# A product-key expert layer: 4 heads x 32 tokens on the partitions, V sums in column groups, and U and V gathered apart

## The chip, the core and the metric

The kernel runs on one core of a Trainium2 chip. The metric is the device time of one execution in microseconds. Everything is fp32 except one attention mask.

## What is computed

Two layers of a decoder trunk on 256 tokens of width 1024: layer 0 is attention (eight MLA heads, eight MoBA heads), layer 1 a conformer convolution (31 taps per channel), and each is followed by PEER, the expert layer that takes most of the time:

```python
q = (xc @ w_q).reshape(128, 8, 2, 128)
s = einsum('thcd,hcnd->thcn', q, subkeys)
s_top, i_top = lax.top_k(s, 16)
cand = s_top[:, :, 0, :, None] + s_top[:, :, 1, None, :]
cand_idx = i_top[:, :, 0, :, None] * 128 + i_top[:, :, 1, None, :]
best, pos = lax.top_k(cand.reshape(128, 8, 256), 16)
idx = take_along_axis(cand_idx.reshape(128, 8, 256), pos, axis=-1)
g = softmax(best)
u, v = u_tab[idx], v_tab[idx]
act = gelu(einsum('td,thkd->thk', xc, u))
return einsum('thk,thkd->td', g * act, v)
```

So every token picks 16 of 16384 experts for each of 8 heads, in both layers: 256 x 8 x 16 x 2 = 65536 pairs of a U row and a V row of 4 KB each, 537 MB that are read once.

## The kernel before

**Tiling.** The 256 tokens are two tiles of 128. An expert *phase* is one tile in one layer: phase 0 and 1 are tile 0 and 1 of layer 0, phase 2 and 3 those of layer 1. A phase has eight heads of 16 *slots*, 512 slots in all. In a slot the 128 partitions are the 128 tokens of the tile, for one head and one of its 16 choices.

**A slot.** GpSimd issues one indirect DMA (`gathers`, L394) that puts each token's row of 8 KB, U beside V, into one of eight buffers of `ring`. VectorE's `dots` (L1237) multiplies the U half with the normed tokens `xn` and sums it into a column of `dot`. ScalarE's `peer_slot` (all of ScalarE's work has L758) applies Gelu, scales it with the gate into `coef`, and scales the identity matrix by it into `diag`. TensorE (all of its matmuls have L407, transposes L413 and L642) multiplies `diag` with the V half, two matmuls of 512 columns, onto `ypsum`, 128 tokens by 1024 columns. Its completion (`ring_free`) lets GpSimd reuse the buffer. `ypsum` is seeded with the tile itself, and VectorE copies it back after 128 slots (`peer_end`, L1324).

**Routing of the next head.** During slots 0 to 3 of a head, TensorE and ScalarE make the next head's queries, their transpose and the key scores (`peer_q`, `peer_qT`, `peer_scores`); during slots 4 to 10 VectorE finds the top 16 and their indices (`route`, L1173 to L1229). SyncE loads one head's weights (1152 KB, `load_head`, L339) as soon as the scores of the head before are done; four heads of layer 1 are loaded once and kept for phase 3.

**What sets the order.** Every engine works through a list written by hand, slot by slot, and waits on semaphores. Work of the other layers is put beside the slots by their number: the second tile's attention beside phase 0 (`beside_attention`, attention head a in slots 25 + 3a to 27 + 3a, the output projection in slots 77 to 82), each tile's convolution beside phases 1 and 2 (`beside_conv`: gated input in slots 7 to 41, taps in slots 16 to 80, norm and output projection in slots 84 to 107), and the norm for the next phase in slots 108 to 111. Between phases all drains: the next phase's first head is routed in the last one.

**Start.** Until the first gather, the first tile's projection and attention run; then the first expert norm, head 0's queries and its route. Two projections of the second tile (`project(1, 1)`, `project(1, 3)`) read weights that lie in the ring and come after head 0's scores.

## Time and profile before

| | us |
|---|---|
| median of 3 runs | 1716.0 |
| lowest and highest | 1713.87, 1719.32 |
| span of the profiled execution | 1710.8 |
| busy: TensorE, VectorE, ScalarE, GpSimd | 1387.0, 1125.6, 727.0, 594.8 |
| first gather issued, first dot | 133.92, 139.58 |
| ends of phases 0 to 3 (copies of `ypsum`) | 563.4, 965.4, 1375.4, 1701.5 |

The span is that of one execution under the profiler; the runs are timed without it. An engine's busy time is the union of its instructions. DMA share is the mean busy share of 16 DMA engines, and PEclk the share of full speed that TensorE's clock was granted. In a row of the timeline, the last bracket is the idle time before the instruction and what ended it.

### The profile page before, as it was taken

The page shows a single profiled execution, that of the slowest core. Times are in us where ns is not written, and L with a number is a line of the kernel's source. Part 1 is how long each engine was busy: PE and PEld are TensorE (multiplying, and loading weights), DVE is VectorE, ACT ScalarE, POOL GpSimd, SP SyncE. Part 2 cuts the span into 40 slices and gives each one's busy share as a digit, 9 for nine tenths or more (in the row PEclk, how much of TensorE's full clock was granted, in tenths as well). Part 3 has the DMA queues.
Part 4 walks back from the last instruction along what each step waited for, and adds up shares of the span by engine and source line. Part 5 has one row for each costly group of instructions (what it writes and reads, how often), then busy time and mean ns, then how long its engine had stood idle before and what let it go on. Part 6 is the DMA issues. An engine that isn't in the chain of part 4 may idle for free.

```text
span 1710.8 us, 17886 instructions
## 1 busy us (share of the span) xinstructions
PE 1387.0 (81%) x4018; PEld 677.3 (40%) x4018; DVE 1125.6 (66%) x3165; ACT 727.0 (42%) x2049; POOL 594.8 (35%) x516
## 2 busy tenths in 40 slices
PE   6998977779587888877888888877877888888886
PEld 3554443434133454423333454433332433333332
DVE  3346746654467758988845758888855666667664
ACT  2313556653234445443443454533443444444442
POOL 0003433333234333433333423344422334544452
PEclk9999999999889999999999999999999899999999
DMA  9108988887999988999998988999988899999996
GB/s 393 43 29 333 421 356 339 318 302 288 426 418 421 421 333 327 362 364 386 400 360 323 421 345 319 362 376 372 378 349 352 345 409 422 423 421 422 412 423 275
DMA packets 82585, 606.81 MB, mean 355 GB/s; under 512 B 9552, under 2 KB 9936, under 8 KB 11600
## 3 DMA queue, kind: packets, MB, share of 16 engines
q0 software_dynamic: 73728, 536.90, 78.5%
q1 hardware_dynamic: 8208, 64.36, 9.2%
q10 hardware_dynamic: 576, 4.72, 0.7%
q8 instruction: 28, 0.46, 0.1%
q14 instruction: 45, 0.37, 0.1%
HBM read 604.89 MB, written 1.05 MB: 354 GB/s over the span
## 4 chain that ended last, share of the span: by engine, by line
PE 42%; DVE 24%; ACT 12%; issue 11%; DMA 8%; DVEq 1%; POOL 1%; SPq 0%; POOLq 0%; ACTq 0%
PE ypsum L407 25%; PE bank L407 8%; DVE ring L1237 8%; DMA ring<-table_dram,idx 8%; PE qpsum L407 7%; ACT L758 4%; DVE arena L1133 4%; ACT diag L758 2%; ACT coef L758 2%; PE spsum L407 1%; ACT gel L758 1%; ACT arena L758 1%; POOL ring L394 1%; DVE topi L1187 1%; DVE sc L1201 1%
## 5 line engine op out<-in xcount | busy, mean ns | idle before, releaser
L407 PE MATMUL ypsum<-ring,diag 128*128 128x512 f32 x2048 | 1021.4, 634 | 287.3 <-ACT diag L758 285.9
L394 POOL DMA_INDIRECT ring<-table_dram,idx x512 | 594.6, 1161 | 1088.3 <-PE ypsum L407 879.4
L1237 DVE CUSTOM_DVE_ANT_0 ring<-xns,ring 128x1024 f32<-128x1024 f32 x512 | 618.2, 1221 | 151.1 <-DMA ring<-table_dram,idx 146.3
L407 PEld LDWEIGHTS ypsum<-ring,diag 128*128 128x128 f32 x2048 | 377.3, 198 | 821.6 <-ACT diag L758 498.8
L758 ACT ACTIVATE gel<-dot 128x1 f32<-128x1 f32 x512 | 102.2, 200 | 524.4 <-DVE dot L1237 503.9
L758 ACT ACTIVATE diag<-ident,coef 128x128 f32<-128x128 f32 x512 | 205.6, 402 | 85.3 <-PE ypsum L407 59.0
L758 ACT ACT_TABLE_LOAD x130 | 166.8, 1283 | 14.9 <-PE bank L413 9.8
L758 ACT ACTIVATE coef<-gel,g_cur 128x1 f32<-128x1 f32 x512 | 150.7, 294 | 16.6
L1133 DVE SCALAR_TENSOR_TENSOR arena<-arena,cols 128x128 f32<-128x128 f32 x480 | 136.5, 347 | 3.4 <-DVE sc L1178 0.7
L1173 DVE MAX8 top<-sc 128x8 f32<-128x128 f32 x64 | 15.6, 285 | 120.1 <-ACT sc L758 120.1
L407 PE MATMUL qpsum<-head,xns 128*128 128x256 f32 x384 | 86.9, 379 | 0.0
L407 PEld LDWEIGHTS qpsum<-head,xns 128*128 128x128 f32 x384 | 73.2, 191 | 20.7 <-issue 12.0
L758 ACT ACTIVATE qq<-qpsum 128x256 f32<-128x256 f32 x32 | 12.3, 385 | 135.5 <-PE qpsum L407 135.5
L407 PEld LDWEIGHTS bank<-hT,arena 128*128 128x128 f32 x512 | 60.0, 192 | 8.7 <-issue 8.7
L407 PE MATMUL bank<-arena,hT 128*128 128x512 f32 (+1 forms) x136 | 59.4, 580 | 0.9 <-ACT hT L758 0.9
L407 PE MATMUL bank<-hT,arena 128*128 128x128 f32 x512 | 59.7, 275 | 0.0
L1237 DVE DVE_READ_ACCUMULATOR2_ANT dot<- 128x1 f32 x512 | 42.3, 83 | 0.0
L1092 DVE TENSOR_SCALAR arena<-bank,arena 128x64 f32<-128x64 f32 x32 | 9.1, 284 | 47.1 <-PE bank L407 46.9
L407 PEld LDWEIGHTS bank<-arena,hT 128*128 128x128 f32 x136 | 26.4, 195 | 32.1 <-issue 30.6
L413 PE MATMUL bank<-ident,arena 128*128 128x128 f32 (+1 forms) x170 | 28.7, 290 | 11.9 <-DVE arena L1032 8.6
L758 ACT ACTIVATE arena<-bank 128x512 f32<-128x512 f32 (+3 forms) x31 | 16.5, 572 | 50.8 <-PE bank L407 48.6
L1086 DVE COPY arena<-bank 128x128 f32<-128x128 f32 (+1 forms) x32 | 11.4, 355 | 40.6 <-PE bank L413 40.5
(132 smaller groups left out, 858.3 us busy)
## 6 DMA issues: line engine op xcount, KB each, us to landing
head<-heads_dram SPq DMA_DIRECT2D x24, 1152.0 KB
ring<-w_in_dram SPq DMA_DIRECT2D x4, 2048.0 KB, 15.7
ring<-table_dram,idx POOLq DMA_INDIRECT x512
arena<-c_in_dram SPq DMA_DIRECT2D x4, 2048.0 KB, 26.4
arena<-heads_dram SPq DMA_DIRECT2D x4, 1152.0 KB
arena<-w_out_dram SPq DMA_DIRECT2D x1, 4096.0 KB, 36.6
arena<-c_out_dram ACTq DMA_DIRECT2D x2, 2048.0 KB, 9.8
xns<-gains_dram SPq DMA_DIRECT2D x5, 512.0 KB, 8.1
```

What stands on the lines that cost most here:

```text
L394: pool.indirect_dma_start(out=ring[:, b * 2 * D:(b + 1) * 2 * D], out_offset=None, in_=table[:, :], in_offset=bass.IndirectOffsetOnAxis(ap ...
L407: return nc.tensor.matmul(o_, l, r, start=start, stop=stop, **kw)
L413: last = nc.tensor.transpose(bank[0:rows_, i * P:(i + 1) * P], s, ident[:, :])
L758: return nc.scalar.activation(out_, in_, func, **kw)
L1086: free(j, V.tensor_copy(pT[a % 2][:, 0:t + 1, :].rearrange("p s t -> p (s t)"), banks[bank_no(j)][:, 0:(t + 1) * P]))
L1092: free(j, V.tensor_scalar(o[:, a * VD:(a + 1) * VD], banks[bank_no(j)][:, 0:VD], rinv[:, a:a + 1], None, ALU.mult))
L1133: own.did(V.scalar_tensor_tensor(out=acc[:, c, :], in0=uT[:, c, bass.ds(k + t * P, P)], scalar=cols[:, bass.ds(k + (C_TAPS + c * TAPS), 1) ...
L1173: own.did(V.max(top_[:, c, 0:8], sc_[:, c, :]))
L1187: own.did(V.max_index(topi_[:, c, 8:16], top_[:, c, 8:16], sc2_[:, c, :]))
L1201: own.then(V.match_replace(cand2[:, :], best[:, 0:8], cand[:, :], low))
L1237: V.tensor_tensor_reduce(out=u, in0=xn[p % 2], in1=u, scale=1.0, scalar=0.0, op0=ALU.mult, op1=ALU.add, accum_out=dot[:, k:k + 1]).then_in ...
```

## The change

1. **Partitions.** A *round* is 16 slots in which the partitions hold 4 heads x 32 tokens. A *group* is 32 tokens, two rounds (heads 0 to 3, then 4 to 7); a phase has four groups, and again 128 slots. The normed tokens are replicated four times for each group: TensorE multiplies them with a 0/1 matrix `rep` into two banks, and ScalarE copies these to `xnr`.
2. **V sums.** ScalarE scales a 128x32 piece of `gident` by the Gelu value into `wts`. `gident` holds the gate times a 32x32 identity under each head; VectorE makes it twice a round (`gates`, eight choices each). `coef` and the copy of the gates fall away. TensorE multiplies each `wts` with four pieces of 256 columns of the V rows, and puts piece j on partitions 32j to 32j+31 of `ypsum`, which so sums the heads as well. Two halves of `ypsum` alternate between groups; ScalarE writes each group back (`take_group`), and VectorE's copy falls away.
3. **Gathers.** `table` becomes `u_table` and `v_table`. A slot has two indirect DMAs of 128 rows of 4 KB. The U ring has six buffers, each free after its dot (`dot_ready`); the V ring has eight, each free after its sum (`v_free`).
4. **Heads.** A round needs the scores of four heads, so all eight heads' queries, transposes and scores are made ahead of a phase: for phase 0 before its first slot, otherwise beside slots 97 to 114 of phase 0 and 107 to 124 of phases 1 and 2, two slots apart. ScalarE copies them, by 32x256 pieces, to where each round's 128 rows lie together. SyncE loads a head in three pieces, each behind the wait that frees its place. Seven heads of layer 1 are kept instead of four.
5. **Beside the slots.** Gated input moves to slots 8 to 64 in halves, taps to slots 17 to 89 by pairs of channel blocks instead of fours, norm and output projection to slots 91 to 103, the next norm to slots 94 and 104. The first gather waits for the three projections whose weights lie in the ring. All loops are unrolled. The second half of the convolution's output weights is loaded by SyncE.

The diff, cut to its core:

```diff
@@ GpSimd
-            def gathers(p, h, last_chunks=False):
-                for k in range(TOPK):
-                    if k % RING == 0:
-                        pool.wait_ge(routed[k // RING], h + (p * HEADS + 1))
-                    b = k % RING
-                    pool.wait_ge(ring_free, h * TOPK + (p * SLOTS + k + 1))
-                    settle(pool)
-                    pool.indirect_dma_start(
-                        out=ring[:, b * 2 * D:(b + 1) * 2 * D], out_offset=None, in_=table[:, :],
-                        in_offset=bass.IndirectOffsetOnAxis(ap=idx[k // RING][:, b:b + 1], axis=0)).then_inc(row_in[b], 16)
+            for n in range(ALL_SLOTS):
+                R, k = divmod(n, TOPK)
+                if k == 0:
+                    pool.wait_ge(routed, R + 1)
+                if n == 0:
+                    for c in (1, 2, 3):
+                        full(pool, PROJ_JOB[1][c])
+                at_ = bass.IndirectOffsetOnAxis(ap=idx[R % 2][:, k:k + 1], axis=0)
+                held(pool, dot_ready, n - U_RING + 1)
+                settle(pool)
+                pool.indirect_dma_start(out=u_row(n), out_offset=None, in_=u_table[:, :], in_offset=at_).then_inc(u_in[n % U_RING], 16)
+                held(pool, v_free, n - V_RING + 1)
+                pool.indirect_dma_start(out=v_row(n), out_offset=None, in_=v_table[:, :], in_offset=at_).then_inc(v_in[n % V_RING], 16)
@@ TensorE
-            def peer_slot(H, k, stop=False):
-                pe.wait_ge(diag_ready, H * TOPK + (k + 1))
-                b = k % RING
-                for half in range(2):
-                    last = mm(ypsum[:, half * CHUNK:(half + 1) * CHUNK], diag[:, (k % 2) * P:(k % 2 + 1) * P],
-                              ring[:, b * 2 * D + D + half * CHUNK:b * 2 * D + D + (half + 1) * CHUNK], False, stop,
+            def add_slot(n):
+                G = n // GROUP_SLOTS
+                pe.wait_ge(v_in[n % V_RING], 16 * (n // V_RING + 1))
+                pe.wait_ge(wts_ready, n + 1)
+                w = wts[:, n % WTS * QT:(n % WTS + 1) * QT]
+                for j in range(QUAD):
+                    last = mm(y_of(G, j), w, v_row(n, slice(j * DQ, (j + 1) * DQ)), False, n % GROUP_SLOTS == GROUP_SLOTS - 1,
                               skip_group_check=True)
-                last.then_inc(ring_free, 1)
+                last.then_inc(v_free, 1)
+            def replicate(G):
+                for j, half in zip(rep_jobs(G), range(2)):
+                    bank = bank_of(pe, j)
+                    g = G % GROUPS
+                    mm(bank[:, :], rep[:, g * P:(g + 1) * P], xn[:, half * CHUNK:(half + 1) * CHUNK], True, True)\
+                        .then_inc(bank_full[bank_no(j)], 1)
+            def beside_heads(p, s):
+                if s == NORM_SLOT[p - 1] + 2:
+                    turn_input(p)
+                for h in range(HEADS):
+                    H, a = p * HEADS + h, s - head_slot(p, h)
+                    if a == 2:
+                        head_scores(H)
+                    if h == 2 and a == 0:
+                        replicate(p * GROUPS)
+                    if a == 0:
+                        head_queries(H)
+                    if a == 1:
+                        head_turn(H)
@@ TensorE, ahead of slot 0
+            turn_input(0)
+            head_queries(0)
+            head_turn(0)
+            head_queries(1)
+            head_scores(0)
...
+            head_turn(3)
+            head_scores(3)
             project(1, 1)
             project(1, 3)
+            for h in range(4, HEADS):
+                head_queries(h)
+                if h > 4:
+                    head_scores(h - 1)
+                head_turn(h)
+            head_scores(HEADS - 1)
@@ SyncE
+            def load_head(H):
+                layer, h = H // (TILES * HEADS), H % HEADS
+                held(sp, head_taken, H)
+                sp.dma_start(head[:, 0:HEAD_A], heads_in[layer][:, h * HEAD_W:h * HEAD_W + HEAD_A]).then_inc(head_a_in, 16)
+                if H:
+                    full(sp, q_job(H - 1))
+                sp.dma_start(head[:, HEAD_A:HEAD_K], heads_in[layer][:, h * HEAD_W + HEAD_A:h * HEAD_W + HEAD_K]).then_inc(head_b_in, 16)
+                if H:
+                    full(sp, s_job(H - 1))
+                sp.dma_start(head[:, HEAD_K:HEAD_W], heads_in[layer][:, h * HEAD_W + HEAD_K:(h + 1) * HEAD_W]).then_inc(keys_in, 16)
@@ ScalarE
-                own.then(run(coef[:, k:k + 1], gel[:, k:k + 1], scale=g_cur[:, k:k + 1]))
-                if not (first and k < 2):
-                    act.wait_ge(ring_free, H * TOPK + (k - 1 + RING))
-                run(diag[:, (k % 2) * P:(k % 2 + 1) * P], ident[:, :], scale=coef[:, k:k + 1]).then_inc(diag_ready, 1)
+                if k == 0:
+                    act.wait_ge(gates_ready, 2 * R + 1)
+                if k == TOPK // 2:
+                    act.wait_ge(gates_ready, 2 * R + 2)
+                if n >= WTS:
+                    act.wait_ge(v_free, n - WTS + 1)
+                run(wts[:, n % WTS * QT:(n % WTS + 1) * QT], gident[:, k * QT:(k + 1) * QT], scale=gel[:, k:k + 1]).then_inc(wts_ready, 1)
@@ VectorE
                 if part_ == 0:
-                    dve.wait_ge(s_copied, H + 1)
+                    emptied(dve, s_job(p * HEADS + (r % PER_GROUP + 1) * QUAD - 1))
+            def gates(R, half):
+                if half == 0:
+                    dve.wait_ge(exp_ready, R + 1)
                     own.then(V.reciprocal(e_inv[:, :], e_sum[:, :]))
+                m = TOPK // 2
+                if R:
+                    dve.wait_ge(wts_ready, (R - 1) * TOPK + (half + 1) * m)
+                V.scalar_tensor_tensor(
+                    out=gident[:, half * m * QT:(half + 1) * m * QT].rearrange("p (k t) -> p k t", k=m),
+                    in0=ident32[:, :].unsqueeze(1).to_broadcast([P, m, QT]), scalar=e_inv[:, 0:1],
+                    in1=e_g[:, half * m:(half + 1) * m].unsqueeze(2).to_broadcast([P, m, QT]),
+                    op0=ALU.mult, op1=ALU.mult).then_inc(gates_ready, 1)
```

## Rows read from the trace of the kernel before

**Rows 1.** The page: busy us of each engine, and GB/s in 40 slices
```profile
PE 1387.0 (81%) x4018; PEld 677.3 (40%) x4018; DVE 1125.6 (66%) x3165; ACT 727.0 (42%) x2049; POOL 594.8 (35%) x516
GB/s 393 43 29 333 421 356 339 318 302 288 426 418 421 421 333 327 362 364 386 400 360 323 421 345 319 362 376 372 378 349 352 345 409 422 423 421 422 412 423 275
```
**Rows 2.** Stretches: start:end length, busy us (instructions) per engine, PEclk, DMA share, GB/s
```profile
213.00:388.00 175.00, 132.98 (x402) 66.91 (x400) 100.94 (x276) 104.43 (x237) 56.56 (x50) 0.95 0.87 329
388.00:425.00 37.00, 36.87 (x104) 18.57 (x105) 13.79 (x27) 10.95 (x39) 10.16 (x10) 1.00 0.74 281
425.00:563.40 138.40, 102.19 (x231) 42.76 (x229) 80.89 (x213) 50.92 (x154) 51.35 (x45) 0.90 1.01 420
563.40:965.40 402.00, 329.74 (x1012) 164.62 (x1012) 299.42 (x860) 176.79 (x493) 147.14 (x128) 0.97 0.93 366
617.00:812.00 195.00, 157.74 (x471) 77.55 (x470) 170.85 (x518) 85.65 (x235) 72.83 (x63) 0.95 0.91 355
864.00:965.40 101.40, 84.45 (x217) 38.52 (x215) 58.80 (x153) 36.59 (x112) 37.03 (x33) 0.98 0.91 358
965.40:1375.40 410.00, 333.48 (x1012) 165.98 (x1012) 299.03 (x860) 176.67 (x493) 146.47 (x129) 0.95 0.91 358
1375.40:1701.50 326.10, 272.36 (x670) 121.12 (x670) 216.96 (x532) 139.86 (x440) 147.99 (x121) 0.98 0.99 412
```
**Rows 3.** Groups by form: line, engine, operation, tiles, shape, count, busy us, mean ns
```profile
L407 PE MATMUL ypsum<-ring,diag 128*128 128x512 f32 x2048 | 1021.4, 634 | 287.3 <-ACT diag L758 285.9 <-issue 0.6
L1237 DVE CUSTOM_DVE_ANT_0 ring<-xns,ring 128x1024 f32<-128x1024 f32 x512 | 618.2, 1221 | 151.1 <-DMA ring<-table_dram,idx 146.3 <-DVE pos L1210 1.1 <-DVE arena L1045 0.4
L394 POOL DMA_INDIRECT ring<-table_dram,idx x512 | 594.6, 1161 | 1088.3 <-PE ypsum L407 879.4 <-DVE idx L1222 133.5 <-issue 75.4
L758 ACT ACTIVATE diag<-ident,coef 128x128 f32<-128x128 f32 x512 | 205.6, 402 | 85.3 <-PE ypsum L407 59.0 <-ACT coef L758 0.2
L758 ACT ACTIVATE coef<-gel,g_cur 128x1 f32<-128x1 f32 x512 | 150.7, 294 | 16.6
L1133 DVE SCALAR_TENSOR_TENSOR arena<-arena,cols 128x128 f32<-128x128 f32 x480 | 136.5, 347 | 3.4 <-DVE sc L1178 0.7 <-DVE sc L1201 0.7 <-DVE pos L1210 0.7
L407 PE MATMUL qpsum<-head,xns 128*128 128x256 f32 x384 | 86.9, 379 | 0.0
L1194 DVE TENSOR_TENSOR sc<-top 128x256 f32<-128x256 f32 x32 | 13.4, 418 | 0.0
```
**Rows 4.** Two stretches: 8 KB gathers in phase 3; the output's 4 KB rows alone
```profile
1400.00:1430.00 30.00, 27.22 (x72) 13.31 (x71) 17.97 (x36) 14.84 (x47) 12.74 (x12) 0.94 1.01 422
1708.00:1711.00 3.00, 0.00 (x0) 0.00 (x0) 0.00 (x0) 0.00 (x0) 0.00 (x0) 0.50 0.43 175
```
**Rows 5.** Timeline, start us and us: a free issue; then dots and a held one
```profile
135.29 0.94 POOL L394 DMA_INDIRECT ring<-table_dram,idx  x1 [0.30 <-issue]
...
1498.02 1.23 DVE L1237 CUSTOM_DVE_ANT_0 ring<-xns,ring 128x1024 f32<-128x1024 f32 x1 [1.17 <-DMA ring<-table_dram,idx]
1498.45 1.59 POOL L394 DMA_INDIRECT ring<-table_dram,idx  x1 [0.78 <-PE ypsum L407]
1500.50 1.23 DVE L1237 CUSTOM_DVE_ANT_0 ring<-xns,ring 128x1024 f32<-128x1024 f32 x1 [1.25 <-DMA ring<-table_dram,idx]
```
**Rows 6.** The chain of work that ended last, beside attention: start us, us
```profile
279.95 0.41 ACT diag L758
...
280.41 1.98 PE ypsum L407 x4
```
**Rows 7.** Timeline of the start: head 0's queries, the first gather
```profile
117.82 3.62 PE L407 MATMUL qpsum<-head,xns 128*128 128x256 f32 x16
...
133.92 1.07 POOL L394 DMA_INDIRECT ring<-table_dram,idx  x1 [133.46 <-DVE idx L1222]
```
**Rows 8.** The loads of the gains (512 KB, L335): time to landing
```profile
DMA to landing us min/median/max: 3.6/8.1/9.5
```

More of the change, by code:

```diff
@@ L194, in build @@
         sel = sb("sel", 2 * TOPK)
[L195 removed]
+        idx = [sb(f"idx{i}", TOPK, u32) for i in range(2)]
         nbest = sb("nbest", 1)
@@ L261, in held @@
         def held(eng, signal, count):
-            if not (isinstance(count, int) and count == 0):
+            if count > 0:
                 eng.wait_ge(signal, count)
@@ new lines, in head_turn, with head_scores @@
+            def head_turn(H):
+                take(t_job(H), q_T, 2 * P)
+            def head_scores(H):
+                p, h = divmod(H, HEADS)
+                hq, i = divmod(h, QUAD)
+                held(act, routed, (p - 1) * ROUNDS + (GROUPS - 1) * PER_GROUP + hq + 1)
+                j = s_job(H)
+                full(act, j)
+                for g in range(GROUPS):
+                    last = run(scores_of(g * PER_GROUP + hq, slice(i * QT, (i + 1) * QT)), banks[bank_no(j)][g * QT:(g + 1) * QT, 0:2 * KEYS])
+                free(j, last)
```

759 lines of the change are left out of this document (378 added, 381 removed).

## The prediction

> **What bounds the kernel now.** I read the page's busy times first [rows 1]: no engine is full, TensorE leads with 81%, and the slices of the DMA run from 29 to 426 GB/s. So the limit changes with the stage, and the second view is the table of stretches [rows 2]. A slot gathers 128 rows of 8 KB (1.049 MB), makes one dot, one weight matrix and one accumulation; there are 512, in four expert phases of 128. The reader is to see three kinds of stage. (a) DMA at 412 to 422 GB/s: the last 45 slots of phase 0 and all of phase 3, where a slot takes 326.1/128 = 2.55 us. (b) Slots 25 to 72, beside attention: 175 us at 329 GB/s, 3.65 us a slot, no engine full; the three compute engines wait for each other in a ring. (c) The tap slots of phases 1 and 2: 195 us for 63 gathers, 3.10 us a slot, with 170.85/63 = 2.71 us of it busy VectorE. TensorE is the limit only in a short piece (388 to 425 us, busy 36.87 of 37). The 1021 us that TensorE spends on ypsum [rows 3] are thus mostly not time that can be won.
>
> **The transfers.** The bytes of a slot stay, in two halves with 4 KB rows. 8 KB gathers fill the DMA at 422/1.01 = 418 GB/s; the 4 KB rows of the output ran at 175/0.43 = 407 [rows 4]. That is a store and a short stretch, but the nearest row: 2.48 us between two dots of a full DMA [rows 5] become 2.48 x 418/407 = 2.55, and with the second completion I take 2.57. Ends: 2.49 (no loss) and 2.70.
>
> **Issuing on GpSimd.** 512 issues become 1024. A free one takes 0.94 us after a gap of 0.30 [rows 5]: two are 2.48 us, just below 2.57. But the issue at 1498.45 took 1.59 us: it began during a dot (1498.02 to 1499.25) and ended 0.79 us after that dot. The mean of all is 1.161 us [rows 3], and twice 1.46 is 2.92 us a slot, above the DMA. Which holds? A U issue waits for a dot's end (`dot_ready`), so it starts as the dot stops: about 0.8 + 0.3, then V's start at 1.1 us, before the next dot (2.57 - 1.23 = 1.34 us after the last), then the next U is held until that dot ends. Two issues fit each dot if nothing slips. I take 2.60 us a slot, nearer the free price because a full ring hides single slips; the other end, 2.92, is a rival.
>
> The row shows the issue held by the dot; the Trainium skill (SBUF — State Buffer, "Who interferes with whom") says that a VectorE instruction with two SBUF inputs contends with a GpSimd one that reads SBUF, and that the second fully blocks. By that rule, the trace agrees. The rule speaks against doubling the issues; it would not choose between 2.60 and 2.92.
>
> **The V sums.** Removed: two fp32 matmuls of 512 columns, 1.98 us a slot [rows 6]. Added: four of 256 columns onto 32 partitions each. One after another they cost four times 86.9/192 = 0.453 us = 1.81; side by side 0.45 [rows 3]. No row uses column groups; I take 0.9, between, and keep both. It counts only where TensorE stands in the ring. Off the path it lifts 1021 us to some 460.
> The Trainium skill (TensorEngine Tiling (Array Packing), "Theoretical Speedup") allows up to fourfold for 32 columns. By it the slot would cost the lower 0.45 and my total fall by about 10 us; no row here shows it.
>
> **ScalarE and VectorE.** `coef` (0.294 us) goes, `diag` (0.402) becomes a scale of 128x32 at perhaps 0.3 [rows 3]: 0.4 us less of each slot's chain. Sixteen replications and the copies of scores and outputs lie beside the DMA. VectorE gains two gate multiplications a round (32 rounds, 0.42 us each by a route's 128x256 operations [rows 3]: 0.05 us a slot) and loses small work; 1.22 us for a dot stays.
>
> **Start.** Now the first head's queries start at 117.82 and the first gather at 133.92 [rows 7]. After, round 0 needs heads 0 to 3. SyncE loads each head in three parts, each queued behind a wait for the head before, and TensorE waits in line: load 4 us, queries 3.6, scores 0.6, 8 us a head for three more; then both remaining projections end before the first gather. I get 160, 26 us later. Then TensorE must finish heads 4 to 7 before its first accumulation, with loads that share the DMA (a 512 KB gain landed in 3.6 to 9.5 us [rows 8]): about 10 us for each of three, to 196. VectorE stops at slot 4, since round 1 wants head 7's scores, and GpSimd stops at its eighth V buffer. From 196, 21 slots x 2.57 put slot 25 at 250, against 213 before: 37 us lost.
>
> **Phase 0, rest.** Slots 25 to 72: a head's ring takes three slots, 175/16 = 10.9 us. It passes one accumulation (1.98 to 0.9) and two to three weighings (0.4 each): 10.9 - 2.2 = 8.7, times 16 = 139 us (before 175). Slots 73 to 82: ten accumulations less by 1.1: 37 becomes 27. Last 45 slots: 47.2 MB of gathers, 10.7 of convolution weights, and now all eight heads of the next phase (9.4 MB, of which the earlier kernel loads two or three here): 67.3 MB at 0.41 MB/us = 164 us, less 10 that full rings hold in store, plus 6 for the chained loads: 160 (before 138.4). Phase 1 starts at 250 + 139 + 27 + 160 = 576 (before 563.4).
>
> **Phases 1 and 2.** First 17 slots at 2.60: 44. Taps now fill 73 slots at 3.4 instead of 3.9 a slot; a tap costs 136.5/480 = 0.284 us [rows 3]. VectorE busy 2.71 - 0.15 + 0.05 = 2.61, with small gaps 2.77: 202 us. Pairs instead of fours stall nothing, as two taps (0.57) outlast one tap's 0.347. Last 38 slots: 39.9 MB, 9.4 of heads, 2.1 of output weights: 125 us, less 10 in store; plus 19 because norm, convolution output and next queries now stand within 17 slots: that chain is about 41 us of work against 44 of transfers, and already ran at 358 GB/s [rows 2]. Phase 1: 44 + 202 + 115 + 19 = 380 (402). Phase 2 has seven kept heads beside its taps (DMA 188 + 20 = 208) and streams no heads at its end: 44 + 208 + 99 + 18 = 369, say 370 (410).
>
> **Phase 3.** 128 x 2.60 = 333 (326.1): a loss of 7. Tail 10 (9.3).
>
> **Sum.** 576 + 380 + 370 + 333 + 10 = 1669 us of span, against 1710.8. The span of the profiled execution lies 5.2 us under the median of the runs, 1716.0 (1713.87 to 1719.32); with about the same around it the time is 1675 us. What is won is 36 us beside attention, 10 in the mixing slots and 62 in the convolution phases; 37 go at the start, 22 at the end of phase 0 and 7 in phase 3.
>
> **Rivals.** (1) GpSimd becomes the bound: mean issues of 1.46 us. For it speaks that the mean issue, 1.161 us, stands 0.22 over a free one though issues now come only once a slot; against it, the lock step above. Price 0.32 us in 128 slots of phase 3 (41), 34 opening slots of phases 1 and 2 (11), 38 closing ones (12), 21 at the start (7), and 0.15 in 146 tap slots (22): 93 us, so 1768, slower. It decides from 2.60 + 0.32 x 41/93 = 2.74 us a slot on. (2) The column groups run one after another: 1.81 instead of 0.9 in 16 rings and 9 mixing slots, 23 us: 1698. TensorE would still not bind: 1.81 is below 2.57. Should the granted clock, 0.98 in phase 3 [rows 2], fall to 1.2 GHz because TensorE has less to do, side-by-side sums of 0.9 us do not bind either. (3) The chained head loads cost 12 us a head rather than 8 at the ends of phases 0 and 1: 16 x 4 = 64 us, 1739, slower; a full V ring (eight slots, 20 us) speaks against it. (4) The added losses of the start and the chains are hidden by rings filled ahead: 1635.
>
> **How the numbers follow.** Forecast 0.44 at 1675; (1) 0.24, (2) 0.12, (3) 0.10, (4) 0.10. All of the forecast, (2) and (4) are faster, 0.66; (1) and (3) are slower but for mild forms near the old time: same 0.06, slower 0.28. A change within 0.3% can't be told from none here. The range, 1630 to 1765, leaves out the fringes of (1) and (4).
>
> **What would show it.** First gather near 160 and first accumulation near 196; in phase 3, dots 2.6 us apart with the DMA above 400 GB/s (right) or 2.9 apart with GpSimd never idle and issues of 1.4 us (rival 1); four matmuls ending within 0.5 to 1 us or over 1.8; slots 25 to 72 in about 139 us; tap slots 2.77 us with VectorE above 90% busy. Most wrong would be a 4 KB gather that moves at well under 400 GB/s, or a start that loses more than 37 us.

## The result, and the profile of the changed kernel

The changed kernel took 1877.4 us (median of four runs, 1864.5 to 1885.3) against 1717.5: a ratio of 1.0918, interval 1.0881 to 1.0955. I had forecast 1675 with a range of 1630 to 1765, and a gain. The same program, measured twice more, took 1803.0 us (1796.4 to 1809.7; ratio 1.0492, 1.0438 to 1.0546) and 1892.5 (1878.1 to 1907.8; 1.1038, 1.0957 to 1.1119). Its run of 1907.8 us counts as slow, and the other three have a median of 1881.0. So the loss has two parts: one of about 85 us that is there each time, and one of 74 to 78 us that was there in two of three measurements. The second and third were made on chips 3 and 12; the chip of the first isn't on record.

The page of the changed kernel, its busy times and its 40 slices of DMA:

```profile
PE 1032.3 (55%) x6242; PEld 489.3 (26%) x6242; DVE 1146.1 (61%) x3162; ACT 616.0 (33%) x1699; POOL 1179.0 (63%) x1028
GB/s 383 15 48 198 256 349 339 341 338 371 415 396 370 369 334 314 352 286 357 363 322 368 372 321 309 335 337 410 404 378 243 301 344 367 356 355 373 350 341 282
```

Against [rows 1], TensorE is down by 355 us, and GpSimd is up from 594.8 to 1179.0. The last eight slices, 409 to 423 GB/s in the kernel before except for the last (275), are at 282 to 373. The groups behind it (line, engine, operation, count, busy us, mean ns of one, then the idle time before them):

```profile
L429 POOL DMA_INDIRECT ring<-u_table_dram,idx x512 | 582.8, 1138 | 410.8 <-issue 324.1
L431 POOL DMA_INDIRECT ring<-v_table_dram,idx x512 | 596.0, 1164 | 270.0 <-issue 137.6
L436 PE MATMUL ypsum<-ring,wts 128*32 128x256 f32 x4096 | 479.7, 552 | 723.7 <-ACT wts L792 425.8
```

The stretches of the changed kernel, cut at slots 0, 25, 73 and 82 of phase 0, at the first dots of phases 1, 2 and 3, and at the last dot (the third row so holds nine of the ten mixing slots 73 to 82, the fourth the tenth and the 45 behind it):

```profile
185.00:283.00 98.00, 54.18 (x312) 27.69 (x312) 57.44 (x168) 31.39 (x91) 57.20 (x49) 0.73 0.86 306
283.00:431.00 148.00, 97.75 (x546) 39.85 (x546) 99.63 (x268) 85.75 (x180) 111.55 (x96) 0.56 0.94 339
431.00:455.00 24.00, 21.13 (x101) 8.62 (x102) 13.41 (x27) 7.42 (x24) 19.06 (x17) 0.78 0.98 367
455.00:622.00 167.00, 90.17 (x576) 47.56 (x578) 85.96 (x218) 52.68 (x160) 89.68 (x88) 0.72 1.01 395
622.00:1050.00 428.00, 234.95 (x1502) 116.97 (x1494) 305.06 (x860) 143.60 (x386) 302.06 (x254) 0.68 0.93 340
1050.00:1486.00 436.00, 243.50 (x1599) 126.33 (x1596) 305.80 (x859) 150.94 (x411) 303.23 (x259) 0.68 0.92 339
1486.00:1863.00 377.00, 146.71 (x1114) 37.90 (x1106) 220.06 (x529) 98.71 (x320) 284.62 (x251) 0.54 0.96 356
```

and of the same program where it took 1803 us, its three last phases:

```profile
615.00:1024.00 409.00, 231.11 (x1504) 116.50 (x1494) 305.68 (x859) 144.45 (x387) 300.63 (x256) 0.68 0.96 356
1024.00:1430.00 406.00, 231.13 (x1600) 119.29 (x1599) 306.18 (x859) 152.30 (x416) 295.29 (x258) 0.71 0.96 364
1430.00:1782.00 352.00, 148.68 (x1100) 35.31 (x1096) 220.58 (x530) 99.36 (x315) 271.05 (x252) 0.53 1.00 382
```

The reader is to see three things against [rows 2]. Phase 3, once 326 us at 412 GB/s, takes 352 and 377 us from its first dot to its last, and no compute engine is near full. GpSimd's busy 271 us in 352 look like slack; but between two issues in a row stand 0.30 us in which it waits for nothing, 252 x 0.31 = 78 us, and 271 + 78 = 349: where the kernel took 1803 us it never waits in phase 3, and is the bound. And attention (slots 25 to 72) is down to 148 us, the ten mixing slots to 29.8 us (461.1 less 431.3). [rows 2] has 175 and 37 for them; cut at the same dots as here, the kernel before has 171.8 (213.5 to 385.3) and 36.0:

```profile
385.30:421.30 36.00, 34.39 (x97) 17.22 (x96) 13.89 (x29) 11.89 (x38) 9.34 (x9) 1.00 0.83 317
1376.90:1697.20 320.30, 268.34 (x663) 119.72 (x663) 214.51 (x529) 138.96 (x437) 147.22 (x121) 0.98 1.00 417
```

The second row is its phase 3, cut alike: 320 us. From here on, a time per slot in phase 3 is the time from its first dot to its last over 127 steps: 2.52 us before, 2.97 in the profile of 1877 us, 2.77 in that of the 1803 us measurement. The expectations below divide by 128 or take [rows 2]'s cut, and say 2.55 and 2.95.

### The profile page after: what moved, and what is told of

Same layout as the page of the kernel before. It is cut to its first block, busy times and chain, and to the rows that moved or that the text cites. A ratio compares the mean times of both kernels' runs of the same rounds, so it can differ in the third digit from the quotient of the medians.

```text
span 1875.7 us, 20918 instructions
## 1 busy us (share of the span) xinstructions
PE 1032.3 (55%) x6242; PEld 489.3 (26%) x6242; DVE 1146.1 (61%) x3162; ACT 616.0 (33%) x1699; POOL 1179.0 (63%) x1028
## 4 chain that ended last, share of the span: by engine, by line
issue 24%; DVE 19%; PE 18%; POOL 16%; DMA 14%; ACT 4%; another core or an unknown queue 4%; SPq 0%; POOLq 0%; DVEq 0%; ACTq 0%
POOL ring L431 8%; POOL ring L429 8%; DMA ring<-u_table_dram,idx 8%; DVE ring L1297 7%; PE bank L436 7%; PE qpsum L436 5%; PE ypsum L436 4%; DMA head<-heads_dram 3%; DVE arena L1185 3%; ACT L792 2%; PE spsum L436 1%; PE bank L441 1%; ACT wts L792 1%; DMA arena<-c_out_dram 1%
## 5 line engine op out<-in xcount | busy, mean ns | idle before, releaser
L436 PE MATMUL ypsum<-ring,wts 128*32 128x256 f32 x4096 | 479.7, 552 | 723.7 <-ACT wts L792 425.8
L429 POOL DMA_INDIRECT ring<-u_table_dram,idx x512 | 582.8, 1138 | 410.8 <-issue 324.1
L431 POOL DMA_INDIRECT ring<-v_table_dram,idx x512 | 596.0, 1164 | 270.0 <-issue 137.6
L436 PEld LDWEIGHTS ypsum<-ring,wts 128*32 128x32 f32 x4096 | 116.7, 131 | 1046.5 <-issue 713.5
L792 ACT ACTIVATE wts<-gident,gel 128x32 f32<-128x32 f32 x512 | 164.6, 321 | 54.9 <-remote 32.5
L436 PE MATMUL qpsum<-head,hT 128*128 128x256 f32 x400 | 118.0, 457 | 51.7 <-DMA head<-heads_dram 50.9
L436 PEld LDWEIGHTS qpsum<-head,hT 128*128 128x128 f32 x400 | 90.1, 232 | 76.3 <-issue 47.7
L436 PE MATMUL bank<-hT,arena 128*128 128x128 f32 x512 | 91.7, 349 | 2.7 <-issue 2.7
L792 ACT ACTIVATE ring<-spsum 32x256 f32<-32x256 f32 x128 | 47.9, 374 | 24.3 <-PE spsum L436 13.9
L436 PE MATMUL bank<-arena 128*128 128x64 f32 (+4 forms) x160 | 47.5, 410 | 0.0
```

The costliest lines, as they stand in the source:

```text
L429: pool.indirect_dma_start(out=u_row(n), out_offset=None, in_=u_table[:, :], in_offset=at_).then_inc(u_in[n % U_RING], 16)
L431: pool.indirect_dma_start(out=v_row(n), out_offset=None, in_=v_table[:, :], in_offset=at_).then_inc(v_in[n % V_RING], 16)
L436: return nc.tensor.matmul(o_, l, r, start=start, stop=stop, **kw)
L792: return nc.scalar.activation(out_, in_, func, **kw)
```

## Experiments: is it the doubled issues?

**b_split.** The kernel before, its row of 8 KB gathered as two of 4 KB into the same buffer.

```diff
-out=ring[:, b * 2 * D:(b + 1) * 2 * D], ... in_=table[:, :], ...).then_inc(row_in[b], 16)
+out=ring[:, b * 2 * D:b * 2 * D + D], ... in_=u_table[:, :], ...).then_inc(row_in[b], 16)
+pool.indirect_dma_start(
+    out=ring[:, b * 2 * D + D:(b + 1) * 2 * D], ... in_=v_table[:, :], ...).then_inc(row_in[b], 16)
```

> The kernel before with one part of the change alone: each slot's 8 KB gather is made by two issues of 128 rows of 4 KB, U then V, from two tables, into the same eight buffers. Nothing is left out. In the changed kernel phase 3 took 2.95 us a slot against 2.55. Theory A (GpSimd is the bound: two issues a slot at 1.16 us and a 0.30 us gap each, since dots hold some of them up): phase 3 goes to 2.8 to 2.95 us a slot, GpSimd waits for little else there, and the time rises by 60 to 120 us, to 1780 to 1840. Theory B (the DMA moves 4 KB rows slower than 8 KB rows, by 13% as share and GB/s of the changed kernel suggest): also near 2.85 a slot, but with GpSimd waiting for buffers. Theory C (the split costs little and the head loads and the order of the work made the kernel slow): 2.6 a slot and below 1750.

Measured: 1766.9 us, ratio 1.0292 (1.0243 to 1.0341), 51 us. Phase 3 goes from 2.52 to 2.73 us a slot, and the mean issue there is 1.07 us: 2 x (1.07 + 0.30) = 2.74. GpSimd's waits for buffers in it, 138 us before, are gone: no idle time between its issues is over 0.4 us. So theory A has the cause right; the size is less than it expected (2.8 a slot and 60 us at least).

**a_join.** The changed kernel with its two gathers made one of 8 KB, in a ring of seven; all else as changed.

```diff
-U_RING, V_RING = 6, 8
+U_RING, V_RING = 7, 7
-held(pool, dot_ready, n - U_RING + 1)
-pool.indirect_dma_start(out=u_row(n), in_=u_table, ...)
 held(pool, v_free, n - V_RING + 1)
-pool.indirect_dma_start(out=v_row(n), in_=v_table, ...)
+pool.indirect_dma_start(out=ring[:, b * 2 * D:(b + 1) * 2 * D], in_=table, ...)
```

> The changed kernel with one part undone: U and V lie side by side in one table again and come by one gather of 8 KB rows into a ring of seven buffers, each free after its V sum. Nothing is left out. Theories A and B both put phase 3 back to 2.55 to 2.6 us a slot (from 2.95) and take 45 to 50 us off it, and more in the tap slots (3.14 to about 2.85): 1877 becomes 1730 to 1770, with the start (some 60 us late) and the chained head loads left. Theory C keeps it above 1820.

Measured: 1718.7 us, ratio 1.0015 (0.9993 to 1.0036), below the 1730 to 1770 that I expected. Its stretches, cut as above:

```profile
185.00:272.00 87.00, 54.33 (x312) 27.40 (x312) 56.54 (x166) 31.58 (x91) 25.23 (x24) 0.74 0.78 309
272.00:420.00 148.00, 97.92 (x548) 40.15 (x549) 99.92 (x271) 86.44 (x185) 55.01 (x48) 0.56 0.95 355
420.00:440.00 20.00, 16.87 (x87) 6.88 (x87) 12.20 (x24) 6.44 (x20) 9.53 (x8) 0.78 1.00 401
440.00:614.00 174.00, 97.86 (x598) 52.08 (x600) 87.12 (x220) 53.24 (x162) 52.06 (x48) 0.70 0.98 388
614.00:996.00 382.00, 232.63 (x1547) 119.43 (x1538) 302.14 (x860) 147.42 (x398) 160.12 (x125) 0.71 0.96 380
996.00:1379.00 383.00, 227.11 (x1564) 118.52 (x1568) 303.38 (x858) 148.98 (x406) 160.87 (x128) 0.70 0.96 383
1379.00:1705.00 326.00, 148.02 (x1088) 35.30 (x1084) 219.71 (x529) 99.15 (x314) 134.72 (x126) 0.53 1.00 412
```

Phase 3 is back at 412 GB/s. It takes 326 us from first dot to last, 6 more than before; counted from the last dot of phase 2 to its own last dot it is 328.6 us, and 329.7 before. The granted clock is the same 0.53 as in the changed kernel: the low clock of TensorE costs nothing here. Against the 1803 us of the changed kernel the joined one gains 27, 23 and 26 us in the three last phases, and nothing in phase 0. So the doubled issues cost some 84 us (medians; the two profiles are 77 apart), and the rest of the change, gains and losses together, is worth nothing: +3 us, within what can be told from no change. The joined kernel also differs from the changed one in its ring of seven and its one wait; the runs on rings and waits below find at most 16 us for such differences.

**a_halfv and a_halfdot.** In the first V's rows are 2 KB (a quarter of the gathered bytes left out), in the second the dot runs over 512 columns (half of each dot left out). Issues as changed.

```diff
-pool.indirect_dma_start(out=v_row(n), ...)
+pool.indirect_dma_start(out=v_row(n, slice(0, D // 2)), ...)      # a_halfv; table [:, 0:D // 2]
-u = u_row(n)
-V.tensor_tensor_reduce(out=u, in0=xnr[G % 2], in1=u, ...)
+u = u_row(n)[:, 0:D // 2]                                         # a_halfdot
+V.tensor_tensor_reduce(out=u, in0=xnr[G % 2][:, 0:D // 2], in1=u, ...)
```

> The changed kernel with the V rows cut to 2 KB: the second half of each V row is not gathered and the sums use the first half twice, so a quarter of the gathered bytes is left out and the number of issues is the same. Theory A: phase 3 keeps its 2.95 us a slot (2.85 to 2.95), the whole time falls by less than 60 us. Theory B: a slot is 0.79 MB instead of 1.05, phase 3 goes to 2.2 to 2.4 us a slot, and the time falls by over 150 us.

> The changed kernel with dots over the first 512 columns only (half of each product sum is left out): a dot takes about 0.65 us instead of 1.22, issues and bytes are the same. Theory A: a dot holds an issue up half as often and half as long, so the mean issue falls from 1.15 to about 1.0 us and phase 3 from 2.95 to about 2.6 us a slot; the tap slots gain as well, as VectorE has 0.57 us less to do in each; in all 100 to 170 us less. Theory B: phase 3 keeps 2.9 us a slot, and only the tap slots gain.

Measured, one run each: 1792.7 and 1683.3 us. The first is 85 us under 1877 (theory A expected less than 60), the second 194 (100 to 170 expected); against the 1803 us measured later they are 10 and 120 under. The unchanged kernel wasn't measured where these two ran, so phase 3 is the safer witness. Phase 3 of a_halfv, then of a_halfdot:

```profile
1407.00:1778.00 371.00, 146.11 (x1102) 35.45 (x1106) 221.03 (x529) 100.33 (x318) 291.93 (x253) 0.54 0.83 273
```

```profile
1340.00:1670.00 330.00, 145.27 (x1084) 35.27 (x1084) 154.10 (x530) 98.42 (x312) 243.53 (x250) 0.54 1.02 406
```

With a quarter fewer bytes phase 3 is no shorter (371 us, DMA at 273 GB/s; its mean issue is 1.16 us, and 2 x (1.16 + 0.31) = 2.94, measured 2.93): the transfers are not the bound. With shorter dots it is 330 us at 406 GB/s, 2.60 us a slot: half a dot less of work on VectorE, which was not full, makes the mean issue 0.98 us instead of 1.08 to 1.14. The price of 4 KB rows by themselves is at most the step from 412 to 406 GB/s.

## Experiments: what holds an issue

In phase 3 of the changed kernel (the profile of 1877 us) 251 issues can be sorted by where they begin against a dot of 1.22 us (worked out from the rows of GpSimd and VectorE):

```
issue begins              issues   mean us   its end, after the dot's end
up to 0.3 before the dot      44      0.94   -
0.0 to 0.1 into it             6      1.45   -
0.1 to 0.5                    41      1.73   0.81
0.5 to 1.0                    32      1.27   0.81
1.0 to 1.1                    28      1.00   0.81
1.1 to 1.3                    16      0.94   -
in no dot                     84      0.95   -
```

The timeline shows the extremes; first the worst place, then the good one (start us, us):

```profile
1521.59 1.22 DVE L1297 CUSTOM_DVE_ANT_0 ring<-xns,ring 128x1024 f32<-128x1024 f32 x1 [2.27 <-DMA ring<-u_table_dram,idx]
1521.67 1.97 POOL L429 DMA_INDIRECT ring<-u_table_dram,idx  x1 [0.30 <-issue]
...
1590.12 0.94 POOL L431 DMA_INDIRECT ring<-v_table_dram,idx  x1 [0.30 <-issue]
1590.34 1.23 DVE L1297 CUSTOM_DVE_ANT_0 ring<-xns,ring 128x1024 f32<-128x1024 f32 x1 [1.33 <-DMA ring<-u_table_dram,idx]
1591.36 1.01 POOL L429 DMA_INDIRECT ring<-u_table_dram,idx  x1 [0.31 <-issue]
1592.67 0.94 POOL L431 DMA_INDIRECT ring<-v_table_dram,idx  x1 [0.30 <-issue]
```

The rows look as if an issue were held at one point, 0.94 - 0.81 = 0.13 us after it begins: if a dot is under way then, the remaining 0.81 us start when the dot ends. The start of a dot is an exception: of the six issues that begin up to 0.1 us into one, three were held and three took 0.94 us, and none that begins up to 0.3 us before one was held. At 1590.12 an issue begins 0.22 us before the dot and goes through, and the dot isn't longer for it (1.23). At 1590 two issues fit into 2.55 us, just as I had forecast; but the place slips, and one issue in the wrong place costs up to 1.0 us. The mean issue is what decides: 2 x (1.135 + 0.31) = 2.89 us a slot here, 2 x (1.078 + 0.31) = 2.78 where the kernel took 1803 us. Measured are 2.97 and 2.77; the first has 15 us in waits of GpSimd on top, told of below.

**a_onein.** The dot replaced by a sum over the U row alone, which reads one operand and writes no product.

```diff
-V.tensor_tensor_reduce(out=u, in0=xnr[G % 2], in1=u, ..., accum_out=dot[:, k:k + 1])
+V.tensor_reduce(dot[:, k:k + 1], u, AX.X, ALU.add)
```

> The changed kernel with the dot replaced by a plain sum over the U row: VectorE reads one operand of 1024 elements from SBUF instead of two, at about the same duration, and writes no product; the output is not the reference's. Theory A with the hold caused by the second SBUF operand: free issues of 0.94 us everywhere, GpSimd waits for buffers again, phase 3 at 2.57 us a slot and DMA at 409 GB/s, total about 1725 plus or minus 20. Rival (any VectorE instruction of that length on SBUF holds the issue): mean issue stays at 1.14, phase 3 at 2.9, total 1870.

Measured, in one run: 1703.0 us, at the lower edge of the expected 1725 plus or minus 20, and below the kernel before and the joined one. So 1024 issues cost nothing by their number as long as they aren't held. Its timeline in phase 3, then of its page the group of U's issues and the slices of the DMA:

```profile
1563.49 0.94 POOL L429 DMA_INDIRECT ring<-u_table_dram,idx  x1 [0.30 <-issue]
1563.73 1.22 DVE L1297 TENSOR_REDUCE dot<-ring 128x1 f32<-128x1024 f32 x1 [1.33 <-DMA ring<-u_table_dram,idx]
1564.73 0.94 POOL L431 DMA_INDIRECT ring<-v_table_dram,idx  x1 [0.30 <-issue]
```

```profile
L429 POOL DMA_INDIRECT ring<-u_table_dram,idx x512 | 492.7, 962 | 454.0 <-issue 302.6
GB/s 383 56 25 94 313 354 409 359 336 357 420 408 405 358 408 409 398 397 395 394 407 325 347 408 409 401 389 409 409 406 329 338 405 408 409 409 409 410 409 285
```

The instruction lasts as long as the dot, and all 389 issues that began in the first 1.1 us of one took 0.93 to 0.95 us. The DMA stands at 409 GB/s in most slices behind the start; with 4 KB rows no slice of phase 3 is over 410 in any run here. The run takes away two things, the second operand and the written product. Other instructions of this run, which had an issue 0.13 us old while they ran, point to the operand: MATCH_REPLACE8 (one operand of full length beside eight values a partition, 128 or 256 elements written) held none of 13, whereas the second TENSOR_TENSOR of the route (two operands, 128x512) held all 22, with the same 0.81 us after its end. No run takes away the product alone. The Trainium skill (SBUF — State Buffer, "Who interferes with whom") says of this chip's reduction that it never contends, and of two SBUF inputs that they contend with a GpSimd instruction that reads SBUF. By that rule, if the issue counts as such an instruction, the trace agrees on both. It also calls the shared pair of ports an exclusive lock, which whoever issues first has for the whole instruction; here a dot that begins after an issue takes its usual 1.23 us, and the measurement decides.

**Rings and waits.** I then asked whether the release of U's issue by the dot's end brings it into step with the dots, or U's ring of six is too short.

```diff
-U_RING, V_RING = 6, 8
+U_RING, V_RING = 7, 7            # a_uring7; a_u8v6: 8, 6; a_u6v7: 6, 7, one buffer unused
-held(pool, dot_ready, n - U_RING + 1)
+held(pool, v_free, n - U_RING + 1)      # a_vwait alone, with 7, 7
```

> The changed kernel with both rings seven buffers long and U's issue waiting for the accumulation (v_free, seven slots back) instead of the dot (dot_ready, six back). Same issues, same bytes. Theory A (issues are held whenever they overlap a dot, whatever released them): phase 3 stays at 2.90 to 2.95 us a slot, total 1870 to 1880. Theory L (the lock step is the harm: a U issue released by a dot's end falls in step with the dots so that V's issue meets the next one; the split kernel with the old waits has 2.71 us a slot): phase 3 falls to about 2.71, 24 to 30 us less there and about 60 in all, 1815.

> The changed kernel with rings of 7 and 7 instead of 6 and 8, and U's issue released by the dot as in the change: the run with 7 and 7 and the accumulation's wait took 1815.9 us. Theory R (the length of U's ring is what counts: with six buffers GpSimd has to wait during the routing slots, seven times 1.8 us in phase 3, and since it is the bound each wait is lost): as with the other wait, 1805 to 1830 us, phase 3 at 2.80 to 2.85 us a slot, GpSimd waiting for nothing there. Theory L (being released by the dot's end is what counts): stays near 1877, phase 3 at 2.90 or more.

> The changed kernel with V's ring shortened from eight buffers to seven (the eighth left unused), U's kept at six; with 7 and 7 the time was 1809.9 us. Theory R (U's ring of six is too short to ride over the routing slots): no better than the changed kernel, 1870 to 1900 us, as V's ring is shorter on top. Theory V (it is V's ring of eight, or where its buffers lie, that brings the stalls): 1800 to 1830 us.

> The changed kernel with eight U buffers and six V buffers, 14 as before. Theory R (only the shorter ring counts, and V's is filled after U's and freed after it): 1850 to 1900 us, because V's six buffers hold V's issue and all that follows until the accumulation six slots back. Theory V (the eighth V buffer did the harm): 1800 to 1830 us. If U's length alone counts, 1800 or less.

Measured: a_vwait 1815.9 us (1.0589, 1.052 to 1.0658), a_uring7 1809.9 (1.0556, 1.0501 to 1.0611), a_u6v7 1814.4 (1.0577, 1.054 to 1.0615), a_u8v6 1819.4 (1.0604, 1.0568 to 1.064). The first two looked like a clean 60 us, first for the wait and then for the ring. They were neither: the unchanged program belongs beside them, and it took 1803.0 on the chip of the last three (a_vwait ran on another, where the unchanged program wasn't measured).

**a_again and a_again2** are the changed kernel itself, a_join2 the joined one beside the second.

> The changed kernel itself, unchanged, profiled once more. In its first profile several engines wait at the same moments for a releaser that the rows don't show (GpSimd 24 times, 36.5 us in all; ScalarE, VectorE too), which no other kernel's profile has. If these stalls belong to the kernel they come again (30 to 45 us on GpSimd, time 1865 to 1885). If they are an accident of that profile, GpSimd's rows show named releasers, the time stays at 1865 to 1885, and GpSimd's waits for buffers are still some 60 us more than the 132 us of the kernel with rings of 7 and 7.

> The changed kernel once more, unchanged, beside the joined one on the same chip. The first measurement gave 1877 us (1864.5 to 1885.3), the second 1803 (1796.4 to 1809.7), from the same program. If the second is the kernel's own time and the first held stalls that don't belong to it: 1795 to 1815 us, no waits for a releaser that isn't shown. If the kernel has two ways of running: either value, or both.

> The joined kernel on the same chip: 1715 to 1722 us as before, so that two issues a slot instead of one cost 80 to 90 us in this kernel (51 in the kernel before), of them 26 in phase 3 (2.75 against 2.55 us a slot), the rest beside the taps and the head loads.

Measured: 1803.0, 1892.5 and 1723.3 us (1.0024, 1.0007 to 1.0041). The first is outside of the 1865 to 1885 that I expected in either case. So no ring and no wait matters by more than 16 us against it, none is faster, and both theories, the lock step and the short ring, fall. The third measurement of the changed kernel shows the second part of the loss again; the joined kernel beside it on the same chip doesn't have it. Waits of the first profile, and a stretch of a_again2 (columns: us in total, times, longest; start us, us):

```profile
POOL ring L431 <- remote: 32.5, 19, 3.0
POOL ring L429 <- remote: 4.0, 1, 4.0
```

```profile
1344.56 0.93 POOL L429 DMA_INDIRECT ring<-u_table_dram,idx  x1 [0.31 <-issue]
1347.32 1.31 DVE L1185 SCALAR_TENSOR_TENSOR arena<-arena,cols 128x128 f32<-128x128 f32 x4 [3.63 <-remote]
1348.31 0.94 POOL L431 DMA_INDIRECT ring<-v_table_dram,idx  x1 [2.82 <-remote]
1349.81 0.20 ACT L792 ACTIVATE gel<-dot 128x1 f32<-128x1 f32 x1 [7.01 <-DVE dot L1297]
```

VectorE stops for 3.6 us inside a chain of its own work, and other engines at the same time, for a releaser that the profile doesn't show. Such gaps in VectorE's own chains are in both profiles of 1876 us: about ten of 1 to 4 us in each, 19 and 15 us in all, ahead of instructions that follow within 0.2 us in the profile of 1795 us. Waits for a releaser that isn't shown are 20 on GpSimd, 28 on ScalarE and 10 on VectorE in the first profile, 15, 42 and 12 in that of a_again2, none in the profile of 1795 us, nor in any other but a_join2, which has one on ScalarE (5.4 us) and one on GpSimd (2.0). GpSimd's waits that aren't mere issue time are 219 and 222 us in all instead of 155, and its issues together 1179 and 1178 us instead of 1158. As it is the bound, most of that is lost. What stops the engines isn't known; 74 to 78 us go with it. Neither the chip nor the number of issues is shown to be the cause: the other split kernels had no such stops on chips 2, 3 and 5.

## Experiments: the start and the heads

In a_join slot 25 comes at 272.4 us, 59 us later than before (213.5). Its first dot waits here:

```profile
183.95 0.16 DVE L1280 RECIPROCAL e_inv<-e_sum 128x1 f32<-128x1 f32 x1 [21.82 <-ACT e_g L792]
```

The exponential stands in ScalarE's list behind head 5's queries, and their weights come late because the first seven gathers run.

**a_start.** The exponential ahead of head 4; heads 5 to 7 beside slots 1 to 7; the gathers wait only for their own buffer's projection.

```diff
+peer_exp(0)                                     # ahead of head_queries(4)
-for h in range(4, HEADS): head_queries(h); ...
+LATE_HEADS = {1: 5, 3: 6, 6: 7, 7: 8}           # made beside these slots
+FIRST_ROUTE = {8: (0, 1), 9: (2, 3), 10: (4, 5)}
```

> The changed kernel with joined 8 KB gathers (1718.7 us), and the start alone reordered: the first gate exponential stands ahead of head 4 in ScalarE's list, heads 5 to 7 are made beside slots 1 to 7, round 1 is routed in slots 8 to 10, and the first gathers wait only for the projection whose weights lie in their own buffer. Theory S (of the 59 us that slot 25 comes later than before, some 13 are VectorE waiting for an exponential that stands behind head 5's load, 4 the projections, and some 12 the heads 5 to 7 on TensorE ahead of the first accumulation): slot 25 moves from 272 to about 245, all later slots with it, 1692 us. Rival (the start is bound by the loads of heads 5 to 7, which compete with the gathers wherever they stand): only the 13 + 4 us or less come back, slot 25 at 256 or later, 1702 us or more; if the second tile's attention then waits for other work, nothing is kept by slot 73.

Measured: 1714.3 us (0.9984, 0.9956 to 1.0012). The first dot is 16.7 us earlier, slot 25 only 5.6 (266.8), so the rival holds. The rows (TensorE's queries of head 6, the next gather):

```profile
193.51 6.67 PE L437 MATMUL qpsum<-head,hT 128*128 128x256 f32 x16 [8.37 <-DMA head<-heads_dram]
...
202.50 0.94 POOL L431 DMA_INDIRECT ring<-table_dram,idx  x1 [15.60 <-PE ypsum L437]
```

The queries wait for their load, the accumulation stands behind them in TensorE's list, and the gathers behind that. Moving heads doesn't help while each one's load starts only when the one before is done.

**a_second.** Heads 1, 3 and 5 are loaded into the ring's last buffer, free until the seventh gather.

```diff
+wq2_ = ring[:, 12 * D:14 * D]; SECOND_HEADS = (1, 3, 5)
+LATE_HEADS = {1: 6, 4: 7, 5: 8}; FIRST_ROUTE = {6: (0, 1), 7: (2, 3), 8: (4, 5)}
+if n == 6: full(pool, q_job(5))                 # ahead of the seventh gather
```

> The joined kernel with the reordered start (1714.3 us), and a second place for query weights: heads 1, 3 and 5 are loaded into the ring's last buffer (free until the seventh gather), so that a head's weights move while the head before is computed, in the 34 us in which the DMA is now at 75 to 110 GB/s. Heads 6 and 7 stand beside slots 1 and 4, round 1 is routed in slots 6 to 8. Theory S (the start is bound by a chain of loads, which costs most where it competes with gathers): each of heads 1 to 3 takes 6 us instead of 8 to 11, the first gather is issued at about 150 instead of 161, slot 25 starts at about 240 (now 266.8, before the change 213.5), total about 1688 us. Rival (the stages behind take the gain back, or the first accumulations still wait for heads 6 and 7): slot 25 at 255 or later, 1702 us or more.

Measured: 1692.1 us (0.9844, 0.9811 to 0.9878), the fastest kernel that computes everything. The queries of heads 0 to 3 no longer wait, and the first gather comes at 152.7 (expected 150), slot 25 at 244.2 (240):

```profile
118.38 3.69 PE L464 MATMUL qpsum<-head,hT 128*128 128x256 f32 x16 [0.84 <-ACT hT L832]
122.82 3.62 PE L464 MATMUL qpsum<-ring,hT 128*128 128x256 f32 x16
127.19 3.62 PE L464 MATMUL qpsum<-head,hT 128*128 128x256 f32 x16
134.06 3.62 PE L464 MATMUL qpsum<-ring,hT 128*128 128x256 f32 x16
...
152.66 1.07 POOL L458 DMA_INDIRECT ring<-table_dram,idx  x1 [152.21 <-DVE idx L1318]
```

22.6 us less at slot 25 than in a_start, and 22.2 less in the median: what the start gives, the later stages keep. The second buffer isn't alone in this step: heads 6 and 7 and the route of round 1 also stand at other slots than in a_start.

**a_thinheads.** The joined kernel, an eighth of the query weights loaded for phases 1 and 2, the chain of waits kept.

```diff
-sp.dma_start(head[:, 0:HEAD_A], ...)
+sp.dma_start(head[:, 0:HEAD_A // 8], ...)       # H >= HEADS; the second half alike
```

> The joined kernel in which the loads of heads for phases 1 and 2 move an eighth of the query weights, with the same chain of waits; the output is not the reference's. If the ends of phases 0 and 1 are bound by bytes, each gets 16 transfers of 0.46 MB = 7.3 MB / 0.41 = 18 us shorter: 1683. If the chain of waits (transfer, queries, turn, scores in turn) is the limit (my third rival), the slots with heads lose more than that, as each of 16 heads gives back its 4 us of landing: two times 25 to 30 us, 1660 to 1670. If neither, under 10 us each.

Measured: 1694.0 us. The end of phase 0 (slot 82 to the next phase) is 161.5 us instead of 173.4, that of phase 1 (slot 90 on) 126.0 instead of 137.5: 12 us each, less than the 18 of the bytes and the 25 to 30 of a chain that sets the pace. So neither limits these stretches by itself, and the chain least (one run).

## Why the prediction was wrong, step by step

- **Issuing on GpSimd: the step that failed.** I saw the hold, and priced its full form as a rival; but I took 2.60 us a slot because a U issue released by a dot's end would leave the next dot room. Two assumptions were in that. First, that such a wait releases it: in phase 3 GpSimd waits for nothing, so no wait sets where an issue falls. Second, that "a full ring hides single slips": a ring hides nothing when the issues themselves are the bound, and each slip stays. Measured were 2.77 us a slot (and 2.97 in the profile on record), with issues of 1.08 to 1.14 us there and 1.15 to 1.19 in phases 1 and 2, not the free 0.94. Rival 1's "mean issues of 1.46 us" are the issue of 1.161 and the gap of 0.30; its "issues of 1.4 us" leave out that the gap is in them. Against its 1.16 the measured issues are nearly what it says, and shorter only in phase 3. So the rival's mechanism is right, and its turning point of 2.74 was just passed. Its price, 93 us, is near the 84 measured, and in part by luck: measured are 27 and 23 us in phases 1 and 2 and 26 in phase 3, where it has 45 for the first two together, 41 for the third and 7 for the start.
- **The stops of several engines**, which go with 74 us in the measurement on record, were in no row of before, and no step of mine has them. Their cause stays open.
- **Start: too small by 22 us.** I had slot 25 at 250; it is 272.4 with joined gathers, 283.3 in the profile on record. The first gather came at 168.0 (166.3 joined), not 160: heads 1 to 3 follow each other every 8.7 us where I had 8, and both projections end after them. The first accumulation waited behind head 7 as forecast, but until 214.9, not 196: heads 5 to 7 took some 15 us each with the wait for their loads, where I had 10. What I missed is the exponential behind head 5; a_start shows that it is worth little, because the loads set the pace.
- **Beside attention: 148 us for the 139 forecast**, in every kernel of the changed layout but a_halfdot (136). Cut at the same dots the stretch was 172 before, so the ring of waits gave 24 us, not 36. **Mixing slots: right**, 27.4 us joined for 27 (29.8 in the profile on record).
- **End of phase 0:** the last 45 slots took 161 us here, 166 joined, for 160. The rate was lower than mine, 389 GB/s on the mean instead of 410; that the single-buffered heads leave gaps is my reading, no run shows it by itself. The mixing slots and this stretch in the joined kernel:

```profile
419.90:447.30 27.40, 24.27 (x123) 9.69 (x122) 14.44 (x28) 7.51 (x24) 11.18 (x9) 0.84 0.98 393
447.30:613.60 166.30, 90.16 (x560) 49.16 (x560) 84.60 (x215) 52.25 (x158) 50.41 (x46) 0.69 0.98 389
```

- **Phases 1 and 2**, once the issues are joined: 382 and 383 us for 380 and 370. The first is right; of the second, 217 us were tap slots, for 208.
- **Transfers: right.** 4 KB rows run at 406 to 409 GB/s where no dot holds the issues for long, my 407. Phase 3 with them takes 2.60 us a slot (a_halfdot, a_onein), my 2.57.
- **Column groups: right, against rival 2.** The eight matmul records of a slot's sum take 0.64 us at full granted clock and 1.08 us at half, where I took 0.9:

```profile
227.25 0.64 PE L436 MATMUL ypsum<-ring,wts 128*32 128x256 f32 x8
230.33 1.08 PE L436 MATMUL ypsum<-ring,wts 128*32 128x256 f32 x8 [2.44 <-ACT wts L792]
```

- **Rival 3** (12 us a head at the phase ends, 32 us more in each) is refuted by the joined kernel, whose end of phase 0 is 6 us over the forecast and whose phase 1 is 2 us over it; a_thinheads gave back 12 us an end.

Put together for the joined kernel: 1669 + 22 (start) + 9 (attention) + 0 + 6 (end of phase 0) + 2 + 13 (phases 1 and 2) - 4 (phase 3 and tail) = 1717 us of span, measured 1717.8. No term was off by more than 22 us, but nearly all were too small, and their 49 us eat the whole gain of 42 that I had forecast: even with the cost of the doubled issues taken away, the change is worth nothing. The held issues, 84 us on top, then turn nothing into a clear loss. By my own views [rows 5] the held issue was the only one shown of its kind; sorting all 128 issues of phase 3 by their place against the dots, in the trace of before, would have given their mean, 1.23 us, and 2 x (1.23 + 0.30) = 3.06 as an upper end. For an unbiased price it lacked one thing: how often an issue falls into a dot when GpSimd never waits. If it falls anywhere, a dot covers it 1.1 us of 2.6 and holds it for 0.5 us on the mean: 0.94 + 0.42 x 0.5 = 1.15 us, and 2 x (1.15 + 0.30) = 2.90. That sum could have been made blind; measured were 2.77 and 2.97.

## What to carry to other kernels

Before a gather is split, ask what its issue costs with everything that can hold it. Take the mean over all its places beside the other engine's work, not the free price: a queue without slack can't choose its moment. Where a chain of loads feeds a single buffer, the idle stretch ahead of the first gather is the cheap place for a second one (22 us here), and moving the consumers about is not a replacement. And measure the unchanged program again beside the variants before explaining a difference between them: two theories here explained 60 us that came from comparing with a measurement made elsewhere.

## What the runs showed of the hardware

- An indirect DMA of 128 rows takes GpSimd 0.94 us, whether its rows are 8, 4 or 2 KB, and 0.30 us stand between two. A VectorE instruction with two SBUF operands that runs 0.13 us after an issue begins holds it until 0.81 us after that instruction's end (mean of the held ones in phase 3 of the changed kernel: 1.25 to 1.40 us). A TENSOR_REDUCE of the same length, with one operand, held none of 389.
- Four matmuls of 32 columns each on different column groups run side by side in fp32: 0.64 us for a slot's sum at full granted clock, against 1.98 us of the two wide ones before, and against 1.81 for four of 256 columns one after another (four times 0.453).
- TensorE's granted clock was 0.53 in phase 3, nearly all of it at the lower of its two levels (1.2 GHz), with the engine busy 148 of 326 us; before it was 0.98, with 272 of 326 busy. The two kernels differ in TensorE's work, but with joined gathers phase 3 took 328.6 us at 0.53 and 329.7 at 0.98 (last dot to last dot).
- The same program with split gathers took 1803 us on one chip and 1877 and 1893 in two other measurements, there with stops on several engines at once; the joined one took 1718.7 and, beside the 1893, 1723.3. The cause stays open.
